# First attention of a two-layer diffusion block in batches of a latent query tile with a context one

## The reference, cut to what matters

```
def diff_attend(q, k, v, lam):
    s = jnp.einsum('bqhmd,bkhmd->bhmqk', q, k).astype(jnp.float32) * ATTN_SCALE
    p = jax.nn.softmax(s, axis=-1)
    w = (p[:, :, 0] - lam * p[:, :, 1]).astype(v.dtype)
    return jnp.einsum('bhqk,bkhe->bqhe', w, v)
...
    o_l = sweep_query_blocks(lambda qb, kb, vb: diff_attend(qb, kb, vb, lam), q_l, k_all, v_all)
    y_l = finish(o_l)
    y_c = finish(diff_attend(proj_q(h_ctx), k_c, v_c, lam)) if need_ctx else None
```

## Time and profile before

| what | us |
|---|---|
| median of 3 runs | 3701.22 |
| lowest and highest | 3699.37, 5995.77 |
| the profiled execution, own time | 3702.54 |
| its span, first to last instruction | 3700.8 |
| the attention stage that changes, in the trace | 259.55 to 442.57 = 183.02 |

### The profile page before, as it was taken

The page is one execution under the profiler, slowest core; times in us unless marked ns, Lnnn a source line. Parts: engine busy times, 40 slices in busy tenths (PEclk is TensorE's granted clock), DMA queues, the critical chain, the costliest instruction groups (busy, mean ns, idle before and its releaser), DMA issues. The chain is left out here.

```text
span 3700.8 us, 52482 instructions
## 1 busy us (share of the span) xinstructions
PE 3563.2 (96%) x19595; PEld 2938.5 (79%) x19595; DVE 2121.7 (57%) x3092; ACT 1336.4 (36%) x2365; POOL 818.7 (22%) x600
## 2 busy tenths in 40 slices
PE   6999999999999999999999999999999989999998
PEld 4877788888888787777778888888878866678886
DVE  5748746556564354444446486565665738855445
ACT  3337632222153473222337431212233334523222
POOL 1510011312223112222120013132110008812222
PEclk9999999999999999999999999999999999999999
DMA  5223123233322204444210123233211240133231
GB/s 192 69 88 139 59 80 116 95 119 108 119 64 69 89 25 148 157 151 151 88 61 2 33 104 115 96 119 108 102 57 57 82 138 18 41 103 103 91 102 68
DMA packets 164785, 344.43 MB, mean 93 GB/s; under 512 B 8732, under 2 KB 18429, under 8 KB 164605
## 3 DMA queue, kind: packets, MB, share of 16 engines
q1 hardware_dynamic: 160493, 332.98, 26.6%
q10 hardware_dynamic: 4144, 9.44, 0.7%
HBM read 333.75 MB, written 12.85 MB: 94 GB/s over the span
## 5 line engine op out<-in xcount | busy, mean ns | idle before, releaser
L594 POOL TENSOR_TENSOR x<-x,scaled_buf 128x512 f32<-128x512 f32 (+1 forms) x360 | 492.8, 1384 | 2103.6 <-DVE scaled_buf L586 2102.9
L132 DVE TENSOR_TENSOR w_lo<-raw,w_hi 128x2048 fp32r<-128x2048 f32 x198 | 465.6, 2352 | 677.0 <-ACT w_hi L126 667.9
L126 ACT ACTIVATE w_hi<-raw 128x2048 fp32r<-128x2048 f32 x197 | 377.1, 1914 | 1282.2 <-PE psum L407 1279.7
L405 PE MATMUL psum<-hT_hi,w_hi 128*128 128x512 f32 (+1 forms) x1888 | 668.4, 354 | 2.9 <-issue 1.7
L406 PE MATMUL psum<-hT_lo,w_hi 128*128 128x512 f32 (+1 forms) x1888 | 665.3, 352 | 0.0
L407 PE MATMUL psum<-hT_hi,w_lo 128*128 128x512 f32 (+1 forms) x1888 | 665.0, 352 | 0.0
L405 PE MATMUL psum<-w_hi,uT_hi 128*128 128x512 f32 x1280 | 503.6, 393 | 0.2
L407 PE MATMUL psum<-w_hi,uT_lo 128*128 128x512 f32 x1280 | 499.0, 390 | 0.0
L406 PE MATMUL psum<-w_lo,uT_hi 128*128 128x512 f32 x1280 | 498.6, 389 | 0.0
L586 DVE TENSOR_TENSOR scaled_buf<-psum,gate 128x512 f32<-128x512 f32 x360 | 245.0, 688 | 327.6 <-PE psum L407 284.6
L405 PE MATMUL psum<-w_hi,hT_hi 128*128 128x512 f32 x1072 | 420.6, 392 | 3.3 <-issue 3.3
(11 more groups left out here) (311 smaller groups left out, 4639.5 us busy)
## 6 DMA issues: line engine op xcount, KB each, us to landing
raw<-in_w_mlp SPq DMA_DIRECT2D x64, 1024.0 KB, 5.3
raw<-in_ff_w SPq DMA_DIRECT2D x64, 1024.0 KB, 5.2
mod_wide<-in_w_mod SPq DMA_DIRECT2D x32, 1536.0 KB, 8.6
mod_wide<-in_w_mod SPq DMA_DIRECT2D x8, 3072.0 KB, 10.6
raw<-in_ssm_w_in SPq DMA_DIRECT2D x20, 1024.0 KB, 5.1
mod_slab<-in_w_mod SPq DMA_DIRECT2D x8, 2048.0 KB, 8.0
raw<-in_a_w_qkv SPq DMA_DIRECT2D x12, 1024.0 KB, 5.2
raw<-in_b_w_qkv SPq DMA_DIRECT2D x12, 1024.0 KB, 5.2
```

What stands on the lines that cost most here:

```text
L126: act.activation(K.w_hi[h][:, :, :], K.raw[h][:, :, :], ACT.Copy).then_inc(K.hi_done.h, 1)
L132: dve.tensor_tensor(K.w_lo[h][:, :, :], K.raw[h][:, :, :], K.w_hi[h][:, :, :].bitcast(F32), ALU.subtract).then_inc(K.lo_done.h, 1)
L405: pe.matmul(out, hi_a, hi_w, start=first, stop=False, **check)
L594: pool.tensor_tensor(x, x, K.scaled_buf[:, j % 2, :], ALU.add).then_inc(K.added.h, 1)
```

## The change

`attention_stage` and the class `Unit` go, and `pair_attention_stage` comes in. It computes the same with the same products. The 48 units become 32 batches: for each pair the tiles (0, 4), (1), (2, 5), (3). In a batch of two, head `m` of the latent tile has columns 0 to 767 of `S[m]`, and that of the context tile columns 768 to 1023. TensorE's scores of a batch now wait once, for VectorE's reads of all heads and tiles of the batch before; VectorE's reads wait for the scores of the whole batch. The inverses and the ratio of a batch are one operation each, with up to four and two elements. Turned blocks (eight or six) lie in banks 4 and 5 and are copied in two parts; both tiles of a batch are multiplied into bank 6 and handed over once. The scores run three batches ahead (`LEAD`) where they ran four units ahead. The modulation products come in the step of the first batch of a pair and are turned in that of the third; VectorE sums them at the head of the fourth. `mod_row` has another place in SBUF.

```diff
-    ahead = 4 if diff else 3
+    batches = [(p, tiles) for p in range(PAIRS) for tiles in ((0, 4), (1,), (2, 5), (3,))]
+    LEAD = 3
+    spans = [slice(0, TOK_TILES * P), slice(TOK_TILES * P, 8 * P)]
...
-                        if col == 0 and not u.masks:
-                            pe.wait_ge(K.s_read.h, at(K.s_read, 2 * (v - 1) + m))
...
+            def scores(b):
+                p, tiles = batches[b]
+                pe.wait_ge(*upto(K.s_read, 2 * units_to[b]))
+                for i, t in enumerate(tiles):
+                    for first, count in ((0, LAT_TILES), (LAT_TILES, 2))[i:]:
+                        at = spans[i].start + (first - keys_of(i)[0]) * P
+                        for m in range(2):
+                            rows = slice(m * HEAD_DIM, (m + 1) * HEAD_DIM)
+                            mm = pe.matmul(S[m][:, at:at + count * P], K.qkv[rows, t, p * P:(p + 1) * P],
+                                           K.qkv[rows, first:first + count, D + p * P:D + (p + 1) * P], start=True, stop=True,
+                                           skip_group_check=True)
+                    mm.then_inc(K.s_done.h, 1)
...
+            for s in range(-LEAD, NB):
...
+                if s >= 0:
+                    turns(s)
+                if s + LEAD < NB:
+                    scores(s + LEAD)
+                if s >= 0 and s % 4 == 0:
+                    modulation_rows(s // 4)
+                if s >= 1:
+                    weighted(s - 1)
+                if s >= 0 and s % 4 == 2:
+                    modulation_columns(s // 4)
...
+            def minima(b):
+                tiles = batches[b][1]
+                if b >= 3:
+                    dve.wait_ge(*upto(K.pt_done[0], 2 * (b - 2)))
+                for i in range(len(tiles)):
+                    dve.wait_ge(*upto(K.s_done, units_to[b + 1]))
+                    for m in range(2):
+                        dve.tensor_scalar(K.p_pair[:, b % 3, m, spans[i]], S[m][:, spans[i]], 1.0, 3e38, ALU.mult, ALU.min,
+                                          accum_out=K.pair_min[:, b % 3, i, m:m + 1]).then_inc(K.s_read.h, 1)
+
+            def joins(b):
+                n = len(batches[b][1])
+                dve.wait_ge(*upto(K.p_done, 2 * units_to[b + 1]))
+                dve.wait_ge(*upto(K.o_read, b - 2))
+                sums, inverse = K.pair_sum[:, b % 3, 0:n, :], K.pair_inv[:, b % 3, 0:n, :]
+                link(dve.reciprocal(inverse, sums))
+                link(dve.scalar_tensor_tensor(inverse[:, :, 1], sums[:, :, 0], K.neg_lam[:, 0:1], inverse[:, :, 1], ALU.mult, ALU.mult))
+                for i in range(n):
+                    w = K.p_pair[:, b % 3, 0, spans[i]]
+                    dve.scalar_tensor_tensor(w, K.p_pair[:, b % 3, 1, spans[i]], K.pair_inv[:, b % 3, i, 1:2], w, ALU.mult, ALU.add)\
+                       .then_inc(K.w_done.h, 1)
...
+            for s in range(-LEAD, NB):
+                if s >= 0 and s % 4 == 3:
...
+                    mod_sums(K, dve, MB, 4).then_inc(K.mod_summed.h, 1)
...
+                if 0 <= s + 1 < NB:
+                    joins(s + 1)
+                if s + LEAD < NB:
+                    minima(s + LEAD)
+                if s >= 1:
+                    finish(s - 1)
...
-            attention_stage(K, [Unit(p, t, every if t < LAT_TILES else [4, 5]) for p in range(PAIRS) for t in mixed], q_of, k_of,
...
+            pair_attention_stage(K, Modulation(0, A["w_mod"][0], 2 * KD))
```

More of the change, by code:

```diff
@@ L1547, in dve_sums @@
             dve.tensor_tensor(out, out, swapped, ALU.add).then_inc(K.rotated.h, 1)
[L1550 to L1577, removed]
 def bias_of(K, p):
@@ L1705, in turn_stage, with pair_attention_stage @@
     K.src_read[1].n += len(items) // 2
-def attention_stage(K, units, q_of, k_of, values, out, diff=False, sink=False, mod=None, squares=False):
+def pair_attention_stage(K, mod):
     nc = K.nc
-    N = len(units)
-    heads = 1 if diff else 2
-    ahead = 4 if diff else 3
[L1718 to L1723, removed]
-    S = [K.psum[:, 2 * m:2 * m + 2, :].rearrange("p a b -> p (a b)") for m in range(2)]
[L1725 to L1734, removed]
@@ new lines, in pair_attention_stage @@
+    batches = [(p, tiles) for p in range(PAIRS) for tiles in ((0, 4), (1,), (2, 5), (3,))]
+    NB = len(batches)
+    LEAD = 3
+    units_to = [sum(len(tiles) for _, tiles in batches[:b]) for b in range(NB + 1)]
+    base = {s: s.n for s in (K.s_done, K.s_read, K.p_done, K.w_done, K.o_done, K.o_read, K.sq_done, K.pt_done[0], K.pt_read[0],
+                             K.mod_used, K.row_out, K.mod_turned, K.mod_summed, K.mod_added, K.mod_loaded[0])}
+    upto = lambda s, count: (s.h, base[s] + count)
@@ L1750, in _ @@
         @block.tensor
         def _(pe):
[L1752 to L1761, removed]
@@ L1784, in weighted, with turns @@
[L1784 to L1803, removed]
+            def turns(b):
+                p, tiles = batches[b]
+                blocks = blocks_of(tiles)
+                for c in range(2):
+                    part = range(4 * c, min(4 * c + 4, len(blocks)))
+                    pe.wait_ge(*upto(K.w_done, units_to[b] + blocks[part[-1]][0] + 1))
+                    pe.wait_ge(*upto(K.pt_read[0], 2 * b + c - 1))
+                    for n in part:
+                        mm = pe.transpose(TB[c][:, (n - 4 * c) * P:(n - 4 * c + 1) * P], K.p_pair[:, b % 3, 0, n * P:(n + 1) * P], K.ident[:, :])
+                    mm.then_inc(K.pt_done[0].h, 1)
@@ L1818, in _ @@
-            for s in range(-ahead, N):
+                pe.wait_ge(K.src_read[e].h, turned[e] - 2)
+            for s in range(-LEAD, NB):
                 if s == 0:
@@ L1846, in probabilities @@
[L1846 to L1854, removed]
-                    p = p_mat[:, v % ahead, u.span(m)]
-                    act.activation(p, p, ACT.Exp, bias=K.neg_max[:, v % 4, m:m + 1],
-                                   scale=-1.0, accum_out=K.p_sum[:, v % 4, m:m + 1]).then_inc(K.p_done.h, 1)
@@ L1859, in squared, with copied @@
-            def squared(v):
-                u = units[v]
-                act.wait_ge(K.o_read.h, at(K.o_read, v))
-                act.wait_ge(K.sq_done.h, sq0 + v)
-                act.activation(K.square_a[:, :], out(u.pair, u.tile), ACT.Square, accum_out=K.pair_ss[:, u.pair, u.tile:u.tile + 1])\
-                   .then_inc(K.sq_done.h, 1)
+            def copied(b):
+                blocks = blocks_of(batches[b][1])
+                act.wait_ge(*upto(K.o_done, b - 1))
+                for c in range(2):
+                    act.wait_ge(*upto(K.pt_done[0], 2 * b + c + 1))
+                    n = min(4, len(blocks) - 4 * c) * P
+                    act.activation(K.pT_pair[:, b % 2, 4 * c * P:4 * c * P + n], TB[c][:, 0:n], ACT.Copy).then_inc(K.pt_read[0].h, 1)
@@ L1950, in attention_stage @@
[L1950 to L1966 removed]
+            finish(NB - 1)
```

220 lines of the change are left out of this document (72 added, 148 removed).

## The result

The changed kernel took 3678.43 us (median of 5 runs, 3677.92 to 3679.7), the kernel before 3700.84 us in the same comparison; the ratio is 0.994, with a 95% interval of 0.9927 to 0.9953. That is 22.4 us less. In two later sets of runs the same kernel took 3681.34 and 3680.88 us beside 3701.06 and 3701.0 us of before, 19.7 and 20.1 us less. So 20 to 22 us is what the change is worth, and those two times lie just inside the range.

What follows compares the result with a forecast made beforehand. TensorE was taken as the bound, with holes behind VectorE: 8 x 19.65 + 1.0 + 9.3 = 167.5 us for the stage against 183.0, 15.5 us less, giving a median of 3686 us; range 3680 to 3698, about 0.82.

Steps and rivals of the forecast that it cites:

- context scores: TensorE's score products of a context unit, two a pair in the steady part, taken at 0.60 us each, 1.20 us a pair.
- groups of eight: TensorE's turned blocks and value products of a two-tile batch, priced at 0.125 and 0.24 us each: 1.00 and 1.92 us.
- the allowance for a late VectorE step: Steady part: 0.12 us a pair for a step in which VectorE comes late, 1 us in all.
- start and end: Stage's ramp and drain: 6.0 us start, 1.7 us slow clock, 1.6 us end; sum 9.3 us, 0.6 more than before.
- The three waits: TensorE idle behind VectorE's reads of the first batches at the stage's start: about 2.5, 1.9 and 1.6 us, together 6.0.
- the holes of 1.34 us: Context unit's scores held up by VectorE's read, twice a pair; 2 x (1.34 - 0.60) = 1.48 us a pair to go.
- the small waits: Latent scores behind a context unit, 1.68 us against 1.49, twice a pair; 2 x 0.19 = 0.38 us a pair to go.
- New waits: Whether TensorE's scores wait anew for VectorE's reads of a batch: slack 0.1 to 0.3 us a step, thin but positive.
- VectorE's small operations cost nothing: Two fewer small operation pairs a pair, 1.0 us, 8 us of VectorE over the stage, costed at nothing under TensorE's 19.65 us.
- VectorE's waits coming back: Rival: coarser hand-overs make VectorE late in the stage's steps; 3690 to 3698 us, say 3693; chance 0.22.
- Engines that wait in turn: Rival: VectorE's scaling and joining outlast turns and scores, so TensorE and VectorE alternate; about 3729 us; chance 0.06.
- Nothing gained: Rival: steady gain offset by a longer slow clock at the start and late VectorE steps; 3698 to 3704 us; chance 0.10.

Runs made afterwards that it cites:

- the filled start and end: Changed kernel with the first modulation products ahead of batch 3's scores and the last value products in bank 7; 3680.97 us, in a later set 3677.88 us.

## Why the prediction was right or wrong

**The step that failed is the size of TensorE's own work in a pair.** The prediction took context scores at 0.60 us, "nearer the measured row". That row was a group that stands alone, and a group carries 0.20 us once: 0.43 + 0.20 = 0.63. Behind latent scores the same products cost 0.43 us, shown by the new trace (1.92 - 1.49) and by the doubled scores (2.35 - 1.92). The low bound in the text, a third of 1.49 = 0.50, still held a share of the once-a-group cost. The trace of the kernel before had all that was needed: each product has two records, and in the latent group of 307.80 they start at 307.80 and 308.34 for the 512 columns and at 308.76 and 308.98 for the 256. From start to start the inner records take 0.43 us for 512 columns and 0.22 for 256, so 256 columns in two records cost 0.43; the surplus lies at the group's two ends.

By terms, stage forecast 167.5 and measured 161.4 us:

- context scores: 2 x (0.60 - 0.43) = 0.34 us a pair, 2.7 us in all;
- groups of eight: turns 308.13 to 309.10 = 0.97 for 1.00, value products 306.25 to 308.13 = 1.88 (1.89 in most pairs) for 1.92; 2 x 0.06 = 0.12 a pair, 1.0 us. The same error again, in small: a price per block that held a share of a group's;
- the allowance for a late VectorE step, which the prediction set without a row, 1.0 us: not needed;
- start and end: 161.42 - 8 x 19.18 = 8.0 us for 9.3. The three waits came as worked out; the 1.7 us for a slow stretch did not come in this profile, and the rest was 0.4 us over, of which 0.27 is the last products' wait (0.80 us for 0.53).

Together 6.0 us of the 6.1. Outside the stage nothing was forecast, and 1.6 us went with the slow stretch behind it. In the median the forecast missed by 7.6 us (3686 against 3678.4), in the two later sets by about 5. The stage was as short in those sets (161.4 and 161.8 us), so the 6 us missed there are real; only whether the kernel's time falls just outside the range or just inside changed from set to set.

**Mechanism.** Right: the holes of 1.34 us and the small waits were real and went. A hole was 0.72 us of waiting and 0.63 us of products, and both shrank, the wait to nothing and the products to 0.43 us: 2 x (1.34 - 0.43) = 1.82 us a pair, with 0.38 for the small waits and 0.40 for the merged turns and value products, together the 2.6 us measured. The wait came from the place of the context scores behind VectorE's read, not from VectorE's load: with that load cut by 1.9 us a pair the hole stayed at 1.35 us, and with the small operations apart again only 1.2 us of the gain was lost.

**New waits.** Right that the slack is thin and positive. 0.40 us more in every step cost 0.52 a pair, so about 0.27 of each 0.40 was covered on the mean, within the forecast's 0.1 to 0.3. It is uneven: two of the four steps covered all of it, and the delay arose beside the step that has the modulation sums too, for which the prediction counted on TensorE's modulation turns.

**VectorE's small operations cost nothing.** Nearly: they were covered but for 0.15 us a pair. Their price was rightly taken from the row. From start to start an inverse costs 0.20 us here (304.42 to 304.62), of which 0.17 is its own time in the profile: the next operation, which needs its result, begins 0.03 us behind its end. The 60 ns that the Trainium skill gives (Perfetto Trace Analysis, "Optimizing Scalar/DVE Operations") is data-access overhead as time in which the engine is busy, and does not price such a chain.

**Rivals.** VectorE's waits coming back needed a load that this change does not have. Engines that wait in turn did appear, but only with two batches of lead (3738.9 us), and there VectorE waited for ScalarE's exponentials, which is not the way that the rival named. That the lead is needed for them stands nowhere in the prediction. "Nothing gained" failed with the first.

**The range.** Its low end allowed 1.6 us for the context scores (0.50 us each, where 0.43 was measured), 1.7 us for a slow stretch that stays away at the start, and 2 us between runs. It did not allow for the second stretch, behind the stage, to stay away too (1.6 us), nor for the 1.0 us allowance and the prices of the turned blocks and value products (1.0 us) to be too high.

## What to carry to other kernels

Price a product that joins a group by the slope between groups of different width, not by a group that stands alone; the part that comes once a group goes away when groups are merged. A hand-over that waits behind another engine's read is mended by changing what stands between, here by giving small work a place beside the large, rather than by making the other engine lighter or the wait finer. Before counting on the new order, add up both engines in each kind of step: one batch of lead less, with the code otherwise equal, cost 60 us, some 48 of them in the steady pairs and 10.9 in pairs with a stretch at the lower clock.

## What the runs showed of the hardware that was not expected

The granted clock falls to 0.50, the level of 1.2 GHz, for 3 to 7 us at two places near this stage, its start and just behind it, in some executions and not in others of the same kernel: at the start in one of three profiles of the changed kernel. Ahead of a fall at the start TensorE had been waiting repeatedly. The cost depends on the length and on what it falls on. In the changed kernel's third profile a stretch of 3.4 us cost 0.4 us (161.82 against 161.42): the scores and turned blocks under it took 1.3 us more, and TensorE's next wait shrank from 1.61 to 0.73 us. In the first profile with the filled start and end a stretch of 7 us, which fell mostly on scores, cost 2.3 us (162.28 against 160.01). The stages with the small operations apart and with the context scores twice, each with such a stretch, are also 2.3 us over what their pairs explain. The waits themselves are not enough to bring it each time; what decides from one execution to the next stays open.
